# Attention kernel: the inverse softmax sums reach the head's partitions through a row in DRAM

## The chip, the cores and the metric

One core of one Trainium2 chip runs the whole program. The metric is device time in microseconds (us) of one launch, the median of three runs. The engines are named as in the profile: PE is TensorE, PEld its weight loads, DVE VectorE, ACT ScalarE, POOL GpSimd, SP SyncE, and SPq and POOLq are the issues of transfers from SP's and POOL's queues.

## The reference

Two layers, of which the first is "forgetting attention" and the second a gated recurrence. Only the attention is touched by the change. Cut to what matters, for 16 heads of width 64 over 2048 positions:

```python
s = einsum("bhqd,bhkd->bhqk", q, k) + cum[:, :, q0:q1, None] - cum[:, :, None, :q1]
p = softmax(where(causal, s, -inf), axis=-1)
o = einsum("bhqk,bhkd->bhqd", p, v[:, :, :q1])
return einsum("bse,ed->bsd", o * silu(gate), w_out)
```

Each query's softmax needs the sum of its exponentials. The kernel weighs the values with the exponentials themselves and multiplies by the inverse sum afterwards, together with the gate.

## The kernel before

The program is a row of stages: `project` (queries, keys, values, gate), `attend`, `merge`, `project`, `recur`. The change lies in `attend`, which takes about a third of the time.

`attend` works through 16 heads, two to a `pair`. A head has 16 blocks of 128 queries, one to a step, and two blocks make a group: 8 groups to a head, 128 in all. Block i meets only the keys up to its own (causal), so the steps of a head grow from one chunk of scores to four. All engines run over the same steps with fixed lags. For step s, PE computes the scores of block s (`score`), transposes the exponentials of block s - 3 (`turn`) and, in two halves over steps 2g + 5 and 2g + 6, multiplies the values with group g (`weigh`). DVE takes the scores out of PSUM and subtracts the high parts from the transposed blocks (`take`, `low`). ACT makes the exponentials with their sums and the high parts (`exps`, `high`). Values are split in a high and a low part throughout; `ops` has the high products on partitions 0 to 63 and the low ones on 64 to 127.

The sums of a group stand in `den`, one per query, hence one per partition, for two blocks (128 x 2). The product in `ops` has the queries along its columns (64 x 256), so the inverse sums have to be laid out along the columns and repeated on 64 partitions. Before the change this goes as follows. DVE inverts at step 2g + 3 (`invert`, L834). PE, at the end of `weigh`, transposes each inverse column, repeated 128 times, into the second half of `ops` (L716, two to a group). ACT, at the end of step 2g + 7, copies three tiles out of `ops` (`move`): the high product to `att` (L780), the low one to `low_sum` (L781), the spread inverse to `scale` (L782). POOL then does five operations of 64 x 256 per group: it adds the products (L641), multiplies `scale` by the gate (L643), writes the product twice (`yh` at L649, `y` at L650) and subtracts (`yl` at L652). The last of them counts up `y_ready`.

The couplings around it matter. `att`, `low_sum` and `scale` have two buffers, so `move` of group n waits for POOL to have finished group n - 2. SP issues every load and store of the stage from one queue, in order. For each group g it issues the gate tile of group g + 2 (L597), waits for `y_ready` of group g and stores `yh` and `yl` (L608, L609); after the first group of each head it also issues the nine transfers that load the whole next head (L586, L587). So the next head's load starts when POOL has finished group 0 of a head, and the gate tile of group 3 is the next thing in SP's queue behind it. POOL issues no transfers in this stage; in the first `project` it issues sixteen (L229), each of 16 rows of 2 KB.

Of the kernel before, what the change touches and what calls it, by code (L numbers as in the profile page):

```python
# [19 lines left out]
P = 128  # L20
BANK = 512
ALU = mybir.AluOpType
ACT = mybir.ActivationFunctionType
F32 = mybir.dt.float32
# [5 lines left out]
HEAD_DIM = 64  # L30
# [24 lines left out]
def raw(ap):  # L55

    return ap.bitcast(F32)
# [388 lines left out]
def wait(engine, sem, value):  # L446

    if not isinstance(value, int) or value > 0:
        engine.wait_ge(sem, value)
# [7 lines left out]
def attend(nc, stage, qs, ks, vs, gs, cum, ys):  # L457
# [13 lines left out]
    GW = 2 * P  # L471
    STEPS = 2 * QT
    GROUPS = 2 * GT
    PAIRS = D // HEAD_DIM // 2
# [17 lines left out]
    with ExitStack() as ctx:  # L492
        a = Alloc(nc, ctx, stage)
# [4 lines left out]
        val = [a.sb(f"val{i}", [P, QT, P], F32R) for i in range(2)]  # L498
# [1 line left out]
        ph = [a.sb(f"ph{i}", [P, QT, GW], F32R) for i in range(2)]  # L500
        pl = [a.sb(f"pl{i}", [P, QT, GW], F32R) for i in range(2)]
        gate = a.sb("gate", [HEAD_DIM, 4, GW])
        low_sum = a.sb("low_sum", [HEAD_DIM, 2, GW])
        scale = a.sb("scale", [HEAD_DIM, 2, GW])
        att = a.sb("att", [HEAD_DIM, 2, GW])
        y = a.sb("y", [HEAD_DIM, GW])
        yh = a.sb("yh", [HEAD_DIM, 2, GW], F32R)
        yl = a.sb("yl", [HEAD_DIM, 2, GW], F32R)
        least = a.sb("least", [P, ROWS, PB])
        den = a.sb("den", [P, 2, 2])  # L510
        rden = a.sb("rden", [P, 2, 2])
        ident = a.sb("ident", [P, P])
        identb = a.sb("identb", [P, P], BF16)
        mask = a.sb("mask", [P, P], BF16)
        sps = [a.ps(f"sps{i}", [P, BANK]) for i in range(SB)]
        tps = [a.ps(f"tps{i}", [P, PB, P]) for i in range(TB)]
        ops = [a.ps(f"ops{i}", [P, 2, GW]) for i in range(2)]

        waited = a.sem("waited")
        const_ready = a.sem("const_ready")  # L520
# [12 lines left out]
        low_out = a.sem("low_out")  # L533
        weighed = a.sem("weighed")
        rden_ready = a.sem("rden_ready")
        spread = a.sem("spread")
        moved = a.sem("moved")
        summed = a.sem("summed")
        scaled = a.sem("scaled")
        gated = a.sem("gated")  # L540
        y_ready = a.sem("y_ready")
# [81 lines left out]
        @block.gpsimd  # L623
        def _(pool):
            for t in (ident, identb, mask):
                nc.gpsimd.memset(t[:, :], 0.0).then_inc(const_ready, 1)
            pool.wait_ge(const_ready, 3)
            for t in (ident, identb):
                nc.gpsimd.affine_select(out=t[:, :], in_=t[:, :], compare_op=ALU.not_equal, fill=1.0, base=0,
                                        pattern=[[-1, P]], channel_multiplier=1).then_inc(const_ready, 1)  # L630

            nc.gpsimd.affine_select(out=mask[:, :], in_=mask[:, :], compare_op=ALU.is_ge, fill=MASKED, base=0,
                                    pattern=[[-1, P]], channel_multiplier=1).then_inc(const_ready, 1)

            def pair(it):
                for g in range(GROUPS):
                    n = it * GROUPS + g
                    b = g % 2
                    wait(pool, gate_loaded[g % 4], 16 * (it * (GROUPS // 4) + g // 4 + 1))
                    wait(pool, moved, 3 * n + 3)  # L640
                    nc.gpsimd.tensor_tensor(att[:, b, :], att[:, b, :], low_sum[:, b, :], ALU.add)\  # L641
                        .then_inc(summed, 1)
                    nc.gpsimd.tensor_tensor(scale[:, b, :], scale[:, b, :], gate[:, g % 4, :], ALU.mult)\  # L643
                        .then_inc(scaled, 1)
                    wait(pool, y_stored[b], 32 * (it * (GROUPS // 2) + g // 2))
                    wait(pool, scaled, n + 1)
                    wait(pool, summed, n + 1)
                    wait(pool, y_ready, n)
                    nc.gpsimd.tensor_tensor(yh[:, b, :], att[:, b, :], scale[:, b, :], ALU.mult).then_inc(gated, 1)  # L649
                    nc.gpsimd.tensor_tensor(y[:, :], att[:, b, :], scale[:, b, :], ALU.mult).then_inc(gated, 1)  # L650
                    wait(pool, gated, 2 * n + 2)
                    nc.gpsimd.tensor_tensor(yl[:, b, :], y[:, :], raw(yh[:, b, :]), ALU.subtract).then_inc(y_ready, 1)  # L652

            pair(0)
            for it in range(1, PAIRS):
                pair(it)

        @block.tensor
        def _(pe):
# [35 lines left out]
            def weigh(it, g, lo, hi):  # L695

                hp, gh, b = g // GT, g % GT, g % 2
                KT = 2 * gh + 2
                if lo == 0:
                    if isinstance(it, int) and it == 0 and hp == 0:  # L700
                        if gh % 2 == 0:
                            pe.wait_ge(first_val[gh // 2], 16)
                    elif gh == 0:
                        wait(pe, val_loaded[hp], 16 * (it + hp))
                    wait(pe, low_out, it * CH + first[2 * g + 1] + n_chunks[2 * g + 1])
                    wait(pe, moved, 3 * (it * GROUPS + g - 1))
                for kt in range(lo, hi):
                    c0 = P if kt == KT - 1 else 0
                    for t in (ph, pl):
                        mm = nc.tensor.matmul(ops[b][:, 0, c0:GW], val[hp][:, kt, :], t[b][:, kt, c0:GW],  # L710
                                              start=(kt == 0 and t is ph), stop=(kt == KT - 1 and t is pl))
                if hi == KT:
                    mm.then_inc(weighed, 1)
                    wait(pe, rden_ready, it * GROUPS + g + 1)
                    for e in range(2):
                        mm = nc.tensor.transpose(ops[b][:, 1, e * P:(e + 1) * P],  # L716
                                                 rden[:, b, e:e + 1].to_broadcast([P, P]), ident[:, :])
                    mm.then_inc(spread, 1)

            def step(it, s, begun):  # L720

# [33 lines left out]
        @block.scalar  # L755
        def _(act):
            def exps(it, s):

                i, g = s % QT, s // 2
                w = (i + 1) * P  # L760
                wait(act, scores_out, it * CH + first[s] + n_chunks[s])
                wait(act, rden_ready, it * GROUPS + g - 1)
                nc.scalar.activation(probs[s % ROWS][:, 0:w], probs[s % ROWS][:, 0:w], ACT.Exp,  # L763
                                     bias=least[:, s % ROWS, n_chunks[s] - 1:n_chunks[s]], scale=-1.0,
                                     accum_out=den[:, g % 2, s % 2:s % 2 + 1]).then_inc(probs_ready, 1)

            def high(it, s, j):
                i, g = s % QT, s // 2
                if j == 0:
                    wait(act, weighed, it * GROUPS + g - 1)  # L770
                c, n = first[s] + j, width(s, j) // P
                wait(act, turned, it * CH + c + 1)
                nc.scalar.activation(ph[g % 2][:, j * PB:j * PB + n, i % 2 * P:(i % 2 + 1) * P],  # L773
                                     tps[c % TB][:, 0:n, :], ACT.Copy).then_inc(high_out, 1)

            def move(it, g):
                b = g % 2
                wait(act, spread, it * GROUPS + g + 1)
                wait(act, y_ready, it * GROUPS + g - 1)
                nc.scalar.activation(att[:, b, :], ops[b][0:HEAD_DIM, 0, :], ACT.Copy).then_inc(moved, 1)  # L780
                nc.scalar.activation(low_sum[:, b, :], ops[b][HEAD_DIM:P, 0, :], ACT.Copy).then_inc(moved, 1)  # L781
                nc.scalar.activation(scale[:, b, :], ops[b][0:HEAD_DIM, 1, :], ACT.Copy).then_inc(moved, 1)  # L782

            def step(it, s, begun):

                def at(d, run):
                    n = s - d
                    if n >= 0 and n < STEPS:
                        run(it, n)
                    elif n < 0 and begun:  # L790
                        run(it - 1, n + STEPS)
                at(TURN_LAG, lambda t, n: [high(t, n, j) for j in range(n_chunks[n])])
                at(1, exps)
                if (s - TURN_LAG) % 2 == 0:
                    at(TURN_LAG + 3, lambda t, n: move(t, n // 2))

            for s in range(STEPS):
                step(0, s, False)
            for it in range(1, PAIRS):
                for s in range(STEPS):  # L800
                    step(it, s, True)
            for s in range(STEPS, STEPS + 3 + TURN_LAG):
                step(PAIRS - 1, s, False)

        @block.vector
        def _(dve):
# [23 lines left out]

            def invert(it, g):
                wait(dve, probs_ready, it * STEPS + 2 * g + 2)
                wait(dve, spread, it * GROUPS + g - 1)
                nc.vector.reciprocal(rden[:, g % 2, :], den[:, g % 2, :]).then_inc(rden_ready, 1)  # L834

            def step(it, s, begun):
                def at(d, run):
# [756 lines left out]
```

## Time and profile before

| | |
|---|---|
| median of 3 runs | 2558.09 us (2556.62 to 2558.27) |
| the profiled execution, its own time | 2556.05 us |
| its span, first to last instruction | 2553.9 us |
| attention, roughly | 770 to 1632 us of the span |
| PE busy in the whole span | 2409.2 us (94%) |
| POOL busy in the whole span | 622.7 us (24%) |
| one head, steady | 52.9 us, 15 times |

Busy shares are averages over stages. In a timeline each row is one instruction or a run of equal ones: its start, its duration, the engine, line and operation, and in brackets how long the engine sat idle before it and what ended that. PE's instructions overlap, so their pace is read from start to start and not from their durations.

### The profile page before, as it was taken

The page shows a single profiled execution, that of the slowest core. Times are in us where ns is not written, and L with a number is a line of the kernel's source. Part 1 is how long each engine was busy: PE and PEld are TensorE (multiplying, and loading weights), DVE is VectorE, ACT ScalarE, POOL GpSimd, SP SyncE. Part 2 cuts the span into 40 slices and gives each one's busy share as a digit, 9 for nine tenths or more (in the row PEclk, how much of TensorE's full clock was granted, in tenths as well). Part 3 has the DMA queues.
Part 4 walks back from the last instruction along what each step waited for, and adds up shares of the span by engine and source line. Part 5 has one row for each costly group of instructions (what it writes and reads, how often), then busy time and mean ns, then how long its engine had stood idle before and what let it go on. Part 6 is the DMA issues. An engine that isn't in the chain of part 4 may idle for free. (4 is left out here: it accounts for less than half of the span.)

```text
span 2553.9 us, 37956 instructions
## 1 busy us (share of the span) xinstructions
PE 2409.2 (94%) x13921; PEld 2081.5 (82%) x13921; DVE 1352.8 (53%) x2844; ACT 1150.0 (45%) x2132; POOL 622.7 (24%) x739
## 2 busy tenths in 40 slices
PE   8999999999989999999999999699699999992997
PEld 7888889998868888888888888587488888872886
DVE  4232121211017888888888888453336656575443
ACT  2131111111117888888888888400035556565100
POOL 0010000000003554555545555244300000000254
PEclk9999999999998999999999999899899999996999
DMA  6434443332116455444554444455344444444653
GB/s 209 122 91 124 124 124 113 119 108 91 66 61 136 98 122 131 104 98 98 128 128 102 97 99 96 147 203 194 124 153 122 142 144 132 139 125 139 236 193 132
DMA packets 219999, 326.62 MB, mean 128 GB/s; under 512 B 17052, under 2 KB 144092, under 8 KB 213996
## 3 DMA queue, kind: packets, MB, share of 16 engines
q1 hardware_dynamic: 219304, 323.68, 44.3%
q8 instruction: 111, 1.82, 0.3%
q0 software_dynamic: 512, 0.53, 0.1%
q14 instruction: 72, 0.59, 0.1%
HBM read 197.79 MB, written 126.35 MB: 127 GB/s over the span
## 5 line engine op out<-in xcount | busy, mean ns | idle before, releaser
L828 DVE TENSOR_TENSOR at_pl<-at_tps,at_ph 128x512 fp32r<-128x512 f32 (+3 forms) x640 | 370.7, 604 | 30.1 <-ACT at_ph L773 30.1
L773 ACT ACTIVATE at_ph<-at_tps 128x512 fp32r<-128x512 f32 (+3 forms) x640 | 311.5, 527 | 114.5 <-PE at_tps L692 107.4
L323 ACT ACTIVATE pa_stg<-pa_ps 128x512 fp32r<-128x512 f32 (+1 forms) x128 | 76.5, 598 | 634.9 <-PE pa_ps L250 634.9
L692 PE MATMUL at_tps<-at_ident,at_probs 128*128 128x128 f32 x2176 | 338.3, 274 | 0.2 <-DVE at_pl L828 0.2
L710 PE MATMUL at_ops<-at_ph,at_val 128*128 128x256 f32 (+1 forms) x1152 | 325.5, 305 | 2.1 <-DVE at_pl L828 0.5
L763 ACT ACTIVATE at_probs<-at_probs,at_least 128x128 f32<-128x128 f32 (+15 forms) x256 | 307.2, 1200 | 9.1 <-DVE at_probs L819 9.0
L250 PE MATMUL pa_ps<-pa_xh,pa_wh 128*128 128x512 f32 x768 | 299.8, 390 | 3.8 <-DVE pa_wl L376 3.8
L250 PE MATMUL pa_ps<-pa_xh,pa_wl 128*128 128x512 f32 x768 | 298.9, 389 | 0.0
L250 PE MATMUL pa_ps<-pa_xl,pa_wh 128*128 128x512 f32 x768 | 298.8, 389 | 0.0
L710 PE MATMUL at_ops<-at_pl,at_val 128*128 128x256 f32 (+1 forms) x1152 | 295.0, 281 | 0.0
L677 PE MATMUL at_sps<-at_k,at_q 128*128 128x512 f32 (+3 forms) x640 | 272.9, 426 | 19.9 <-DMA at_k<-forget_sums 15.8
L692 PEld LDWEIGHTS at_tps<-at_ident,at_probs 128*128 128x128 f32 x2176 | 256.6, 141 | 22.2 <-DVE at_pl L828 4.1
L819 DVE TENSOR_SCALAR_CACHE_REDUCE at_probs<-at_sps,at_least 128x512 f32<-128x512 f32 (+3 forms) x384 | 248.1, 646 | 16.4
L678 PE MATMUL at_sps<-at_k,at_q 68*128 68x512 f32 (+3 forms) x640 | 233.9, 369 | 0.0
L710 PEld LDWEIGHTS at_ops<-at_ph,at_val 128*128 128x128 f32 x1152 | 221.1, 192 | 12.8 <-DVE at_pl L828 4.4
L710 PEld LDWEIGHTS at_ops<-at_pl,at_val 128*128 128x128 f32 x1152 | 220.1, 191 | 8.3
L1301 PE MATMUL rep_ps<-rep_xh,rep_wh 128*128 128x512 f32 x512 | 201.4, 393 | 3.8 <-DVE rep_wl L1440 3.8
L1301 PE MATMUL rep_ps<-rep_xh,rep_wl 128*128 128x512 f32 x512 | 200.1, 391 | 0.0
L1301 PE MATMUL rep_ps<-rep_xl,rep_wh 128*128 128x512 f32 x512 | 200.0, 391 | 0.0
L959 PE MATMUL rem_ps<-rem_wh,rem_yin 128*128 128x512 f32 x512 | 160.6, 394 | 39.1 <-DMA rem_yin<-y_gated 39.1
L819 DVE TENSOR_SCALAR_CACHE_REDUCE at_probs<-at_sps 128x512 f32<-128x512 f32 (+3 forms) x256 | 162.0, 633 | 64.4 <-PE at_sps L678 60.8
L641 POOL TENSOR_TENSOR at_att<-at_att,at_low_sum 64x256 f32<-64x256 f32 x128 | 93.3, 729 | 385.7 <-ACT at_scale L782 221.7
(172 smaller groups left out, 4645.4 us busy)
## 6 DMA issues: line engine op xcount, KB each, us to landing
at_q<-q_halves SPq DMA_DIRECT2D x45, 512.0 KB
at_k<-k_halves SPq DMA_DIRECT2D x45, 512.0 KB
q_halves<-pa_stg SPq DMA_DIRECT2D x32, 512.0 KB, 3.8
k_halves<-pa_stg SPq DMA_DIRECT2D x32, 512.0 KB, 3.7
v_halves<-pa_stg SPq DMA_DIRECT2D x32, 512.0 KB, 2.8
y_gated<-rep_work SPq DMA_DIRECT2D x32, 512.0 KB, 2.9
at_val<-v_halves SPq DMA_DIRECT2D x15, 1024.0 KB, 17.4
pa_wst<-in_attn_w_in SPq DMA_DIRECT2D x14, 1024.0 KB, 7.2
```

Source lines behind the costliest of these rows:

```text
L250: mm = nc.tensor.matmul(out, lhs[p](c), rhs[q](c), start=(c == 0 and k == 0), stop=(c == KC - 1 and k == 2))
L641: nc.gpsimd.tensor_tensor(att[:, b, :], att[:, b, :], low_sum[:, b, :], ALU.add)\
L677: nc.tensor.matmul(out, q1[hp][:, i * P:(i + 1) * P], k1[hp][:, keys], start=True, stop=False)
L678: mm = nc.tensor.matmul(out, q2[hp][0:K, i * P:(i + 1) * P], k2[hp][0:K, keys], start=False, stop=not last)
L692: mm = nc.tensor.transpose(tps[c % TB][:, k, :], probs[s % ROWS][:, t0:t0 + P], ident[:, :])
L710: mm = nc.tensor.matmul(ops[b][:, 0, c0:GW], val[hp][:, kt, :], t[b][:, kt, c0:GW], start=(kt == 0 and t is ph), stop=(kt == KT - 1 and t ...
L763: nc.scalar.activation(probs[s % ROWS][:, 0:w], probs[s % ROWS][:, 0:w], ACT.Exp, bias=least[:, s % ROWS, n_chunks[s] - 1:n_chunks[s]], sc ...
L773: nc.scalar.activation(ph[g % 2][:, j * PB:j * PB + n, i % 2 * P:(i % 2 + 1) * P], tps[c % TB][:, 0:n, :], ACT.Copy).then_inc(high_out, 1)
L819: nc.vector.tensor_scalar(probs[s % ROWS][:, j * BANK:j * BANK + w], sps[c % SB][:, 0:w], 1.0, least[:, s % ROWS, j - 1:j] if j else None, ...
L828: nc.vector.tensor_tensor(pl[g % 2][at], tps[c % TB][:, 0:n, :], raw(ph[g % 2][at]), ALU.subtract)\
L959: mm = nc.tensor.matmul(psum[u][:, h, :], yin[n // 2 % 4][:, l, c, n % 2 * P:(n % 2 + 1) * P], w[:, c, h * BANK:(h + 1) * BANK], start=(c ...
L1301: mm = nc.tensor.matmul(psum[t % RING][:, :], wt[:, b, k, :], xt[:, k, at], start=(k == 0 and m == 0), stop=(k == KC - 1 and m == 2))
```

## The change

The transposes of the inverse sums on PE (L715 to L718) and the third copy on ACT (L782) go. In their place POOL issues two transfers per group: `store_rden` writes the inverse sums of a group (128 partitions x 2) to a row of 256 numbers in DRAM, and `spread_rden`, after the first has landed, reads that row onto 64 partitions of `scale`. POOL issues the store for group n + 1 at the head of its work on group n, and the spread for group n + 1 between its second and third operation on group n. PE no longer waits for `rden_ready`, and ACT's `move` waits for `weighed`. `att`, `low_sum`, `scale` and `rden` get four buffers, so that `move` of group n waits for group n - 4; `invert` waits until the store of group n - 4 has landed.

```diff
-        ops = [a.ps(f"ops{i}", [P, 2, GW]) for i in range(2)]
+        ops = [a.ps(f"ops{i}", [P, GW]) for i in range(2)]
+        row_scales = nc.dram_tensor("row_scales", (2, 2, P), F32, kind="Internal").ap()
...
+            def store_rden(n):
+                pool.wait_ge(rden_ready, n + 1)
+                pool.dma_start(row_scales[n % 2].rearrange("e p -> p e"), rden[:, n % 4, :], allow_slow_non_contiguous=True)\
+                    .then_inc(rden_stored[n % 2], 16)
+
+            def spread_rden(n):
+                pool.wait_ge(rden_stored[n % 2], 16 * (n // 2 + 1))
+                wait(pool, gated, 2 * n - 6)
+                pool.dma_start(scale[:, n % 4, :], row_scales[n % 2].rearrange("e p -> (e p)").partition_broadcast(HEAD_DIM))\
+                    .then_inc(rden_spread[n % 2], 16)
...
                 for g in range(GROUPS):
                     n = it * GROUPS + g
                     b = g % 2
+                    if n == 0:
+                        store_rden(0)
+                        spread_rden(0)
+                    if n + 1 < GROUPS * PAIRS:
+                        store_rden(n + 1)
                     wait(pool, gate_loaded[g % 4], 16 * (it * (GROUPS // 4) + g // 4 + 1))
-                    wait(pool, moved, 3 * n + 3)
+                    wait(pool, moved, 2 * n + 2)
+                    wait(pool, rden_spread[b], 16 * (n // 2 + 1))
...
+                    if n + 1 < GROUPS * PAIRS:
+                        spread_rden(n + 1)
...
                 if hi == KT:
                     mm.then_inc(weighed, 1)
-                    wait(pe, rden_ready, it * GROUPS + g + 1)
-                    for e in range(2):
-                        mm = nc.tensor.transpose(ops[b][:, 1, e * P:(e + 1) * P],
-                                                 rden[:, b, e:e + 1].to_broadcast([P, P]), ident[:, :])
-                    mm.then_inc(spread, 1)
...
-                wait(act, spread, it * GROUPS + g + 1)
-                wait(act, y_ready, it * GROUPS + g - 1)
+                wait(act, weighed, it * GROUPS + g + 1)
+                wait(act, y_ready, it * GROUPS + g - 3)
...
-                nc.scalar.activation(scale[:, b, :], ops[b][0:HEAD_DIM, 1, :], ACT.Copy).then_inc(moved, 1)
...
-                wait(dve, spread, it * GROUPS + g - 1)
-                nc.vector.reciprocal(rden[:, g % 2, :], den[:, g % 2, :]).then_inc(rden_ready, 1)
+                wait(dve, rden_stored[g % 2], 16 * ((it * GROUPS + g) // 2 - 1))
+                nc.vector.reciprocal(rden[:, g % 4, :], den[:, g % 2, :]).then_inc(rden_ready, 1)
```

## Rows read from the trace of the kernel before

**Rows 1.** The page: busy time by engine, then 40 slices of the span.

```profile
PE 2409.2 (94%) x13921; PEld 2081.5 (82%) x13921; DVE 1352.8 (53%) x2844; ACT 1150.0 (45%) x2132; POOL 622.7 (24%) x739
...
POOL 0010000000003554555545555244300000000254
PEclk9999999999998999999999999899899999996999
```

**Rows 2.** Busy time in stretches: 100 us of attention, then two parts of a head.

```profile
900.00:1000.00 100.00, 99.26 (x745) 89.13 (x743) 85.76 (x240) 86.11 (x182) 53.57 (x75) 1.00 0.48 109
...
841.00:865.00 24.00, 24.00 (x174) 21.63 (x173) 23.51 (x65) 20.70 (x40) 7.51 (x12) 1.00 0.93 199
865.00:894.00 29.00, 28.62 (x222) 25.61 (x221) 22.29 (x65) 25.04 (x59) 21.16 (x30) 1.00 0.15 38
```

**Rows 3.** Timeline of POOL over one head: start us, duration us.

```profile
840.43 0.73 POOL L652 TENSOR_TENSOR at_yl<-at_y,at_yh 64x256 fp32r<-64x256 f32 x1
...
864.83 0.73 POOL L641 TENSOR_TENSOR at_att<-at_att,at_low_sum 64x256 f32<-64x256 f32 x1 [10.86 <-DMA at_gate<-gate_path]
865.53 0.73 POOL L643 TENSOR_TENSOR at_scale<-at_scale,at_gate 64x256 f32<-64x256 f32 x1
867.89 0.73 POOL L652 TENSOR_TENSOR at_yl<-at_y,at_yh 64x256 fp32r<-64x256 f32 x1
868.59 0.73 POOL L641 TENSOR_TENSOR at_att<-at_att,at_low_sum 64x256 f32<-64x256 f32 x1
...
893.37 0.73 POOL L652 TENSOR_TENSOR at_yl<-at_y,at_yh 64x256 fp32r<-64x256 f32 x1
```

**Rows 4.** Timeline of SP's queue in the same head.

```profile
841.25 0.45 SPq L608 DMA_DIRECT2D y_halves<-at_yh  x1
...
845.57 0.60 SPq L586 DMA_DIRECT2D at_k<-k_halves  x1
...
846.87 0.25 SPq L586 DMA_DIRECT2D at_k<-forget_sums  x1
...
847.66 12.96 SPq L597 DMA_DIRECT2D at_gate<-gate_path  x1
```

**Rows 5.** Waits in the attention stage, 770 to 1640 us: total us, times, longest.

```profile
POOL at_att L641 <- ACT at_scale L782: 221.7, 97, 25.8
POOL at_att L641 <- DMA at_gate<-gate_path: 164.0, 15, 11.3
```

**Rows 6.** Timeline of PE at the end of a group.

```profile
1186.83 0.28 PE L710 MATMUL at_ops<-at_pl,at_val 128*128 128x128 f32 x1
1186.94 0.40 PE L716 MATMUL at_ops<-at_ident,at_rden 128*128 128x128 f32 x2
1187.18 0.60 PE L692 MATMUL at_tps<-at_ident,at_probs 128*128 128x128 f32 x4
```

**Rows 7.** Groups of instructions: count, busy us, mean ns, idle before.

```profile
L782 ACT ACTIVATE at_scale<-at_ops 64x256 f32<-64x256 f32 x128 | 48.4, 378 | 3.1
L834 DVE RECIPROCAL at_rden<-at_den 128x2 f32<-128x2 f32 x128 | 20.5, 160 | 9.9 <-ACT at_probs L763 9.9
```

**Rows 8.** The transfers that POOL issues at L229: durations ns min/median/max, then landing.

```profile
L229 POOL DMA_DIRECT2D forget_sums<-pa_fbuf x16: 484/487/672, 150.2 to 183.1; - x16
...
DMA to landing us min/median/max: 1.8/3.4/7.0
```

**Rows 9.** The page: DMA queues, packets, MB and share of 16 engines.

```profile
q1 hardware_dynamic: 219304, 323.68, 44.3%
...
q0 software_dynamic: 512, 0.53, 0.1%
```

**Rows 10.** Timeline of POOL, the last head's group 0 and the last group.

```profile
1581.85 0.73 POOL L652 TENSOR_TENSOR at_yl<-at_y,at_yh 64x256 fp32r<-64x256 f32 x1
...
1627.69 0.72 POOL L652 TENSOR_TENSOR at_yl<-at_y,at_yh 64x256 fp32r<-64x256 f32 x1
```

**Rows 11.** Timeline of PE: the first scores of the next head.

```profile
866.22 0.30 PE L677 MATMUL at_sps<-at_k,at_q 128*128 128x128 f32 x1
```

More of the change, by code:

```diff
@@ L502, in attend @@
         gate = a.sb("gate", [HEAD_DIM, 4, GW])
-        low_sum = a.sb("low_sum", [HEAD_DIM, 2, GW])
-        scale = a.sb("scale", [HEAD_DIM, 2, GW])
-        att = a.sb("att", [HEAD_DIM, 2, GW])
+        low_sum = a.sb("low_sum", [HEAD_DIM, 4, GW])
+        scale = a.sb("scale", [HEAD_DIM, 4, GW])
+        att = a.sb("att", [HEAD_DIM, 4, GW])
         y = a.sb("y", [HEAD_DIM, GW])
@@ L510, in attend @@
         den = a.sb("den", [P, 2, 2])
-        rden = a.sb("rden", [P, 2, 2])
+        rden = a.sb("rden", [P, 4, 2])
         ident = a.sb("ident", [P, P])
@@ L535, in attend @@
         rden_ready = a.sem("rden_ready")
-        spread = a.sem("spread")
+        rden_stored = [a.sem(f"rden_stored{i}") for i in range(2)]
+        rden_spread = [a.sem(f"rden_spread{i}") for i in range(2)]
         moved = a.sem("moved")
@@ L638, in pair @@
                     b = g % 2
+                    if n == 0:
[3 more added lines that the diff above has]
+                        store_rden(n + 1)
                     wait(pool, gate_loaded[g % 4], 16 * (it * (GROUPS // 4) + g // 4 + 1))
-                    wait(pool, moved, 3 * n + 3)
-                    nc.gpsimd.tensor_tensor(att[:, b, :], att[:, b, :], low_sum[:, b, :], ALU.add)\
+                    wait(pool, moved, 2 * n + 2)
+                    wait(pool, rden_spread[b], 16 * (n // 2 + 1))
+                    nc.gpsimd.tensor_tensor(att[:, g % 4, :], att[:, g % 4, :], low_sum[:, g % 4, :], ALU.add)\
                         .then_inc(summed, 1)
-                    nc.gpsimd.tensor_tensor(scale[:, b, :], scale[:, b, :], gate[:, g % 4, :], ALU.mult)\
+                    nc.gpsimd.tensor_tensor(scale[:, g % 4, :], scale[:, g % 4, :], gate[:, g % 4, :], ALU.mult)\
                         .then_inc(scaled, 1)
+                    if n + 1 < GROUPS * PAIRS:
+                        spread_rden(n + 1)
                     wait(pool, y_stored[b], 32 * (it * (GROUPS // 2) + g // 2))
@@ L648, in pair @@
                     wait(pool, y_ready, n)
-                    nc.gpsimd.tensor_tensor(yh[:, b, :], att[:, b, :], scale[:, b, :], ALU.mult).then_inc(gated, 1)
-                    nc.gpsimd.tensor_tensor(y[:, :], att[:, b, :], scale[:, b, :], ALU.mult).then_inc(gated, 1)
+                    nc.gpsimd.tensor_tensor(yh[:, b, :], att[:, g % 4, :], scale[:, g % 4, :], ALU.mult).then_inc(gated, 1)
+                    nc.gpsimd.tensor_tensor(y[:, :], att[:, g % 4, :], scale[:, g % 4, :], ALU.mult).then_inc(gated, 1)
                     wait(pool, gated, 2 * n + 2)
@@ L705, in weigh @@
                     wait(pe, low_out, it * CH + first[2 * g + 1] + n_chunks[2 * g + 1])
-                    wait(pe, moved, 3 * (it * GROUPS + g - 1))
+                    wait(pe, moved, 2 * (it * GROUPS + g - 1))
                 for kt in range(lo, hi):
@@ L709, in weigh @@
                     for t in (ph, pl):
-                        mm = nc.tensor.matmul(ops[b][:, 0, c0:GW], val[hp][:, kt, :], t[b][:, kt, c0:GW],
+                        mm = nc.tensor.matmul(ops[b][:, c0:GW], val[hp][:, kt, :], t[b][:, kt, c0:GW],
                                               start=(kt == 0 and t is ph), stop=(kt == KT - 1 and t is pl))
@@ L777, in move @@
                 b = g % 2
-                wait(act, spread, it * GROUPS + g + 1)
-                wait(act, y_ready, it * GROUPS + g - 1)
-                nc.scalar.activation(att[:, b, :], ops[b][0:HEAD_DIM, 0, :], ACT.Copy).then_inc(moved, 1)
-                nc.scalar.activation(low_sum[:, b, :], ops[b][HEAD_DIM:P, 0, :], ACT.Copy).then_inc(moved, 1)
-                nc.scalar.activation(scale[:, b, :], ops[b][0:HEAD_DIM, 1, :], ACT.Copy).then_inc(moved, 1)
+                wait(act, weighed, it * GROUPS + g + 1)
+                wait(act, y_ready, it * GROUPS + g - 3)
+                nc.scalar.activation(att[:, g % 4, :], ops[b][0:HEAD_DIM, :], ACT.Copy).then_inc(moved, 1)
+                nc.scalar.activation(low_sum[:, g % 4, :], ops[b][HEAD_DIM:P, :], ACT.Copy).then_inc(moved, 1)
             def step(it, s, begun):
```

## The prediction, as it was put on record before the change was run

> **What bounds the kernel now.** I read the page first. PE is busy in 94% of the span and POOL in 24% [rows 1], which makes PE look like the bound and POOL free. The share is an average, so I next cut the attention stage into stretches. Over 100 us of it PE is busy 99.26 us at full clock, DVE 85.76, ACT 86.11 and POOL 53.57 [rows 2]. PE sets the pace, and POOL is twice as full here as in the whole span. In the first 24 us of a head's cycle DVE reaches 23.51 us as well.
>
> Then I followed POOL through one head. Call "the ring" the way from one head's group 0 being finished on POOL to the next head's. It is finished at 841.16 (840.43 + 0.73) and at 894.10 (893.37 + 0.73): 52.94 us [rows 3]. The reader is to see two parts. In the first, up to 864.83, 23.67 us pass, and POOL does groups 1 and 2 and then sits 10.86 us until the gate tile of group 3 is there [rows 3]. The cause is SP's queue: 0.1 us after the group is finished SP starts to store it and then to issue the next head's load, and the gate tile behind it takes 12.96 us to issue [rows 4], while the DMA engines are busy 93% of the time [rows 2]. This happens 15 times, once for each head load [rows 5]. In the second part, from 864.83 to 894.10, 29.27 us, POOL does six groups (3 to 7 and the next head's 0). A group back to back takes 3.76 us (864.83 to 868.59) [rows 3], so six take 22.56 and 6.71 us are idle. That is all the slack POOL has, because the first part starts anew when group 0 is finished and its 23.67 us run from there. More buffers don't add to it: lag is carried over, since the next load starts as much later.
>
> **What is removed.** On PE, two transposes per group. Start to start they take 1187.18 - 1186.94 = 0.24 us, and matmuls stand on either side without a gap [rows 6]; 128 x 0.24 = 30.7 us, or 1.92 us per head, all on the path now as PE is full. DVE's 0.49 us of idle in the 24 us [rows 2] holds back a little of it, as three of the eight groups lie there; I take 1.7 to 1.9. On ACT a copy of 378 ns per group, 48.4 us in all [rows 7], off the path: ACT has 14% idle. It also brings `moved` 0.4 us earlier. Left alone, PE would make the ring about 51.1 us.
>
> **What is added: two issues on POOL per group.** No transfer of this shape is in the trace. The nearest is POOL's own at L229: 487 ns each for 16 rows [rows 8]. I take POOL to be unable to compute meanwhile, as it is an instruction in its order. The new store has 256 pieces of 4 bytes (neighbours in DRAM lie on different partitions), the spread 64 rows. The low bound is 0.49 us for each. The high bound goes by packets: L229's 16 transfers made 512 packets [rows 8, 9], 32 each with the ones that signal, so 15.2 ns a packet; 272 give 4.14 us and 80 give 1.22. Between them I go by how an issue grows on SP: 0.25 us for 2 rows, 0.60 for 64 [rows 4], 5.6 ns a row. From 0.487 that gives 0.487 + 240 x 0.0056 = 1.84 us for the store and 0.76 for the spread. It is another engine's slope, but the one measured slope there is, so I take it.
>
> **What is added: a wait for the store's landing.** The spread of group n + 1 waits on POOL for a store issued at the head of the same round, and the three operations that finish group n are queued behind it; for these wait SP's stores and, for group 0, the next head's load. While PE sets the pace this is hidden, for POOL waits for `moved` anyway. Once POOL is behind, only the store's own issue and two operations cover it (865.53 + 0.73 - 864.83 = 1.43 us) [rows 3]. Landing takes 1.8 us at least and 3.4 in the median [rows 8]. Least: 1.8 is under 0.49 + 1.43, no stall. Median: 3.4 - 1.92 = 1.48. Chosen: issue 1.84, the 1.31 between issue and landing of the quickest at L229, and 16 small packets on each DMA engine. A packet costs 0.443 x 16 x 2553.9 / 219304 = 82 ns [rows 9], so 1.3 us more: 4.45 us, less 1.84 + 1.43, a stall of 1.18. The spread's own landing is covered by the rest of the round (0.76 + 2.33 + 1.84 = 4.9 us).
>
> The Trainium skill (DMA: Bandwidth & Descriptors, Anatomy of one DMA, SWDGE path) gives a fixed cost of about 2.0 us for a small transfer issued from POOL; the trace has 1.8 to 3.4 [rows 8]. By 2.0 and the low issue the sum would be some 2540 us, as in the first rival below. The same page (Rules for kernel authors) says that a strided last dimension becomes one descriptor per element, which speaks against this store. By 256 descriptors the sum is the one below; with one for each of the 128 partitions a group would cost 6.2 us and the whole come to some 2645. No row here shows such a store.
>
> DVE's `invert` now waits for the store of group n - 4, which lies five rounds back on POOL: free until POOL lags by four groups, and then it waits together with `move`. The reciprocal is the same 160 ns [rows 7]. The new transfers carry 1 KB and 64 KB per group and are no load; I cost their bytes at nothing, and if they slowed the head load the 23.67 us would grow.
>
> **The sum.** Group 3 waits for its gate with the store of group 4 already issued, so it costs 3.76 + 0.76 = 4.52. The five others cost 3.76 + 1.84 + 0.76 + 1.18 = 7.54 each. The ring is 23.67 + 4.52 + 5 x 7.54 = 65.9 us against 52.94: 13.0 more, 15 times, 194 us. Groups 1 and 2 of a head fit into 23.67. In the last head seven groups follow with no load; they took 1628.41 - 1582.58 = 45.83 us [rows 10] and take 7 x 7.54 = 52.8, so 7 more. The profiled execution's 2556.05 us (2.0 under the median) becomes 2757; I say 2750. PE's 30 us vanish, because PE waits for POOL. A second ring gives no more: the load lands just before the gate tile, at about 23 us, and PE scores the new head at 866.22, 25.1 us in [rows 11], so a head load that starts late soon stalls PE too, but by less than POOL's own ring.
>
> **The rivals.**
> *POOL keeps up* (faster). At the lowest prices a group costs 3.76 + 0.98 = 4.74, group 3 4.25, and the ring is 23.67 + 4.25 + 23.7 = 51.6. That is 1.3 us less per head, 20 in all, with 1.7 in the last head: 2534 us. For it: the issues at L229 are short, and POOL waits 386 us in the stage [rows 5]. Against: it decides at 5.00 us per group ((52.94 - 27.92) / 5), which leaves 0.26 us for every stall and every piece beyond L229's.
> *Break-even.* Between 4.93 and 5.07 us a group the rings differ by under 0.35 us: 2551 to 2561.
> *Short issues, ordinary landing.* Issues 0.49, landing 3.4 us: a stall of 1.48 and 0.09 for the spread, 6.31 a group, ring 59.5: 98 us more, 2652.
> *Pieces cost by the packet.* 3.76 + 4.14 + 1.22 + 1.18 = 10.3 a group, ring 80.1: 407 us more and 26 in the last head, 2990.
>
> **How the numbers follow.** A measurement of this kernel tells about 0.2% (5 us) from no change. Chances: forecast, 2690 to 2860, 0.37; short issues with ordinary landing, 2590 to 2690, 0.20; by the packet, above 2860, 0.15; slower but under 2590, 0.05; break-even 0.05; POOL keeps up 0.18. Slower is then 0.77. The range goes from 2534, the best that the ring allows, to 2860: outside are the 0.15 above and about 0.03 below. The forecast's own range is 2690 to 2860.
>
> **What would show it.** Right: the heads' cycle is about 66 us, POOL's idle before L641 on `moved` is nearly gone after the gate tile of each head, the spread's issue waits about a microsecond for the landing of the store, and ACT waits at L780 for POOL's `yl`; PE's busy share in the stage falls to about 80%. Wrong: the store's issue is short or its landing is under 2.3 us; the gate tile comes much sooner than 23.67 us after group 0; POOL computes while a transfer is being issued; or the head's cycle is 51 us with PE still at 99%.

## The result, and the profile after

The changed kernel takes 3389.51 us in the median of four runs (3382.6 to 3390.47), the kernel before 2558.18 beside it: a ratio of 1.3245 (95% interval 1.3223 to 1.3268). It is 831 us slower. I had forecast slower with 0.77, but 2750 us, with a range up to 2860. Where a time below comes without a ratio, it is that of a single execution.

The page of the changed kernel, which answers to [rows 1] and [rows 9]:

```profile
span 3388.0 us, 37692 instructions
...
PE 2587.3 (76%) x13665; PEld 2217.0 (65%) x13665; DVE 1370.9 (40%) x2844; ACT 1135.8 (34%) x2004; POOL 783.7 (23%) x995
...
PE   9999999997575565655656656565379699999498
...
PEclk9999999998787776777777777686789899999799
...
q0 software_dynamic: 8704, 9.06, 1.7%
```

PE has fallen from 94% to 76% of a longer span, and the slices show where: the attention stage, in which PE had been full, now runs mostly at five to six tenths, and the granted clock in it falls to 0.6 to 0.8. Project, merge and the recurrence look as before. In the attention stage the waits, in total us, times and longest, say what PE and all others wait for:

```profile
POOL at_scale L647 <- DMA row_scales<-at_rden: 807.4, 117, 10.7
...
DVE at_rden L851 <- DMA row_scales<-at_rden: 417.0, 85, 10.3
...
PE at_sps L700 <- DMA at_k<-forget_sums: 261.1, 16, 20.0
POOL at_att L662 <- DMA at_scale<-row_scales: 137.9, 69, 7.9
...
POOL at_att L662 <- DMA at_gate<-gate_path: 76.3, 14, 9.2
...
POOL at_att L662 <- ACT at_att L798: 10.8, 4, 9.0
```

The first row is the answer. POOL waits 807 us, in 117 of 128 groups, for its own store of the inverse sums to land before it can issue the spread (L647). The wait for ACT's copies, 222 us in [rows 5], has shrunk to 11: POOL is always behind. DVE waits for the same stores at `invert` (417 us), and PE for head loads. ACT, which I had expected to wait at its first copy for POOL's `yl`, did so once, for 9.6 us: with four buffers the delay reaches DVE, ACT and PE through `invert`. One round of POOL, in the part of a head where only this pattern is left:

```profile
1267.56 0.76 POOL L640 DMA_DIRECT2D row_scales<-at_rden  x1
1268.85 0.72 POOL L662 TENSOR_TENSOR at_att<-at_att,at_low_sum 64x256 f32<-64x256 f32 x1 [0.53 <-ACT at_att L798]
1269.53 0.71 POOL L664 TENSOR_TENSOR at_scale<-at_scale,at_gate 64x256 f32<-64x256 f32 x1
1278.32 0.56 POOL L647 DMA_DIRECT2D at_scale<-row_scales  x1 [8.07 <-DMA row_scales<-at_rden]
...
1280.42 0.72 POOL L675 TENSOR_TENSOR at_yl<-at_y,at_yh 64x256 fp32r<-64x256 f32 x1
1281.08 0.76 POOL L640 DMA_DIRECT2D row_scales<-at_rden  x1
```

The store is issued at 1267.56 in 0.76 us. The two operations that can cover its landing are over at 1270.24. The spread is issued at 1278.32, 10.8 us after the store, and the next round begins at 1281.08: 13.5 us for a group that had cost 3.76 [rows 3]. In the median a round takes 12.6 us. Over the 117 groups that waited, the time from the store's issue to the spread's is 9.87 us in the median. I call this the landing from here on; it can be read in each run in the same way.

The other half of the ring got longer too. This is SP's queue behind a head load, to be held against the 12.96 us of [rows 4]:

```profile
1218.36 24.29 SPq L599 DMA_DIRECT2D at_gate<-gate_path  x1
```

From group 0 finished (1210.89 + 0.73 = 1211.62) to the start of group 3 (1246.80) it is now 35.2 us against 23.67. SP got past that issue at 1242.65. By itself this isn't the whole growth: POOL's own groups 1 and 2, each with its wait for a store, and the next store's issue lasted until 1242.95, 31.3 us, so 7.7 of the 11.5 us would have come with a gate tile in time, and POOL waited only 3.86 us more for it.

Why the gate tile is late shows in the traffic. First the changed kernel, in 4 us with a store out (issued at 1211.57, awaited until 1221.77) and the head load issued behind it, then in 4 us after it had landed and the next store had been issued, then in 4 us later on; below it the kernel before at the same place of a head. The columns are the stretch, PE, PEld, DVE, ACT and POOL busy, the clock, the DMA engines' busy share and GB/s:

```profile
1217.00:1221.00 4.00, 2.00 (x15) 1.71 (x14) 0.32 (x2) 2.85 (x6) 0.00 (x0) 1.00 0.83 35
1224.00:1228.00 4.00, 1.67 (x8) 1.27 (x7) 1.79 (x5) 0.60 (x1) 1.28 (x2) 0.50 1.06 244
...
1233.00:1237.00 4.00, 0.00 (x0) 0.00 (x0) 0.00 (x0) 0.00 (x0) 0.00 (x0) 0.50 0.90 102
```

```profile
847.00:851.00 4.00, 4.00 (x30) 3.50 (x29) 3.88 (x10) 3.73 (x10) 0.82 (x2) 1.00 1.05 225
```

35 GB/s against 244 and 225, at a busy share of 0.83: the engines are occupied and move little. The next store is issued at 1224.52, behind a full load. It is out in the second row too, and there the traffic holds; it dips some 9 us later (third row) before POOL sees that store land at 1239.45. So it isn't the mere presence of a store. That its pieces wait their turn behind the load and hold up the rest when it comes is my reading; no view shows single pieces. A head takes 104.6 us in the median of the 15, against 53.0.

### The profile page after: what moved, and what is told of

Its sections match the earlier page's. It is cut to its first block and busy times, and to the rows that moved or that the text cites. A ratio compares the mean times of both kernels' runs of the same rounds, so it can differ in the third digit from the quotient of the medians.

```text
span 3388.0 us, 37692 instructions
## 1 busy us (share of the span) xinstructions
PE 2587.3 (76%) x13665; PEld 2217.0 (65%) x13665; DVE 1370.9 (40%) x2844; ACT 1135.8 (34%) x2004; POOL 783.7 (23%) x995
## 3 DMA queue, kind: packets, MB, share of 16 engines
q1 hardware_dynamic: 219304, 323.68, 38.3%
q0 software_dynamic: 8704, 9.06, 1.7%
## 5 line engine op out<-in xcount | busy, mean ns | idle before, releaser
L700 PE MATMUL at_sps<-at_k,at_q 128*128 128x512 f32 (+3 forms) x640 | 329.5, 515 | 626.2 <-DVE at_probs L836 349.4
L700 PEld LDWEIGHTS at_sps<-at_k,at_q 128*128 128x128 f32 x640 | 151.0, 236 | 664.0 <-DVE at_probs L836 375.6
L715 PE MATMUL at_tps<-at_ident,at_probs 128*128 128x128 f32 x2176 | 407.2, 315 | 3.5 <-DVE at_pl L845 3.4
L733 PE MATMUL at_ops<-at_ph,at_val 128*128 128x256 f32 (+1 forms) x1152 | 363.5, 334 | 2.2 <-DVE at_pl L845 2.1
L733 PE MATMUL at_ops<-at_pl,at_val 128*128 128x256 f32 (+1 forms) x1152 | 327.1, 307 | 0.0
L715 PEld LDWEIGHTS at_tps<-at_ident,at_probs 128*128 128x128 f32 x2176 | 304.9, 164 | 32.4 <-issue 11.1
L701 PE MATMUL at_sps<-at_k,at_q 68*128 68x512 f32 (+3 forms) x640 | 276.3, 435 | 0.0
L733 PEld LDWEIGHTS at_ops<-at_ph,at_val 128*128 128x128 f32 x1152 | 255.5, 222 | 15.5 <-DVE at_pl L845 3.0
L647 POOL DMA_DIRECT2D at_scale<-row_scales x128 | 71.7, 560 | 823.0 <-DMA row_scales<-at_rden 807.4
L976 PE MATMUL ma_ps<-ma_wh,ma_yin 128*128 128x512 f32 x512 | 159.4, 392 | 67.3 <-DMA ma_yin<-y_halves 67.3
```

The source lines that it names most:

```text
L700: nc.tensor.matmul(out, q1[hp][:, i * P:(i + 1) * P], k1[hp][:, keys], start=True, stop=False)
L701: mm = nc.tensor.matmul(out, q2[hp][0:K, i * P:(i + 1) * P], k2[hp][0:K, keys], start=False, stop=not last)
L715: mm = nc.tensor.transpose(tps[c % TB][:, k, :], probs[s % ROWS][:, t0:t0 + P], ident[:, :])
L733: mm = nc.tensor.matmul(ops[b][:, c0:GW], val[hp][:, kt, :], t[b][:, kt, c0:GW], start=(kt == 0 and t is ph), stop=(kt == KT - 1 and t is pl))
L976: mm = nc.tensor.matmul(psum[u][:, h, :], yin[n // 2 % 4][:, l, c, n % 2 * P:(n % 2 + 1) * P], w[:, c, h * BANK:(h + 1) * BANK], start=(c ...
```

## The experiments

Four theories were to be told apart. A: the store's pieces are slow because they are many, small and side by side. B: any transfer issued from POOL lands late here. C: the transposes' removal did harm by itself. D: the ring through the head load and the gate tile, as I had predicted it, was the main limit. All edits are to the changed kernel unless it says otherwise.

**Without the transfers, and with the spread alone.** In the first, neither transfer is issued and `scale` comes from the gate tile alone; in the second the row is stored once.

```diff
-                    nc.gpsimd.tensor_tensor(scale[:, g % 4, :], scale[:, g % 4, :], gate[:, g % 4, :], ALU.mult)\
+                    nc.gpsimd.tensor_tensor(scale[:, g % 4, :], gate[:, g % 4, :], gate[:, g % 4, :], ALU.mult)\
...
-                    if n + 1 < GROUPS * PAIRS:
-                        store_rden(n + 1)
...
-                    if n + 1 < GROUPS * PAIRS:
-                        spread_rden(n + 1)
```

> The changed kernel without any of the 256 transfers: POOL squares the gate tile instead of multiplying it by the inverse sums, so the outputs are not normalised; POOL's five operations, ACT's two copies and PE's shorter groups stay. Both theories (slow store; slow transfers from POOL of any kind) expect PE to set the pace: a head's ring of about 51.1 us, 27 us less than before, 2527 to 2536 us by the profiled execution. If the removal of the transposes itself did harm, it would be at or above 2558.

Measured: 2543.76 us, ratio 0.9947 (0.9930 to 0.9963). C falls: the removal gives 13 us. It gives half of what I had forecast, and the time lies above the 2527 to 2536 that I had expected of this run. The heads take 52.0 us, 1.0 less, not 1.9. In the waits of the steady part (790 to 1580 us), the kernel before and then this run:

```profile
PEld at_sps L677 <- DVE at_probs L819: 11.8, 30, 0.5
```

```profile
PEld at_sps L692 <- DVE at_probs L828: 24.5, 77, 0.6
```

PE's weight loads now wait more than twice as often for DVE to take scores out of PSUM (77 times, not 30), 13 us more in all. DVE, at 23.51 of 24 us in the first part of a head [rows 2], is by this the next bound; no run made DVE's work lighter to show it.

> The row is stored once, for group 0, and every group spreads that same row (so all groups are scaled by group 0's sums): the spread's 128 issues and landings stay, the 127 other stores go. Theory A (the many small writes of the store are slow to be confirmed): a group costs POOL 3.76 + 0.56 = 4.3 us, its ring is 23.7 + 26 = 49.6 us, under PE's 51.1, so 2530 to 2545 us. Theory B (any transfer issued from POOL is slow to land here): the spread is late too, a group costs over 6 us and the time is over 2640 us.

Measured: 2553.94 us, ratio 0.9986 (0.9977 to 0.9996). B falls: 128 spreads of 64 KB issued from POOL leave the heads at 52.0 us. The 10 us over the first run, of which 9 are over the range I expected, lie outside the heads' cycle: the first group is finished 6.3 us later (its last operation starts at 793.84, not 787.59), since POOL first has to see a store land; the last one 3.6 us later; and PE's wait for the merge's first loads is 28.8 us and not 20.8.

**The stores without POOL's wait.** The spreads read another row, so POOL need not wait.

```diff
-                pool.wait_ge(rden_stored[n % 2], 16 * (n // 2 + 1))
...
-                pool.dma_start(scale[:, n % 4, :], row_scales[n % 2].rearrange("e p -> (e p)").partition_broadcast(HEAD_DIM))\
+                pool.dma_start(scale[:, n % 4, :], fixed_row.rearrange("e p -> (e p)").partition_broadcast(HEAD_DIM))\
```

> All stores and all spreads are issued, but the spreads read another row, stored once, and POOL doesn't wait for the stores (only DVE does, four groups later). If the store only takes long to be confirmed (pure latency), a group costs 3.76 + 0.76 + 0.56 = 5.1 us, the ring is 54 us, 2575 us. If the DMA engines also stand still while the small writes are out, eight stores of some 8 us and 21 us of head load no longer fit in 54 us: ring 85 to 105 us, 3050 to 3400 us.

Measured: 2980.67 us, a head 80.6 us in the median. POOL waits for no store here, yet 424 us are lost against the kernel before. That lies between my two expectations: more than latency alone, less than a full standstill. Where POOL and PE wait now:

```profile
POOL at_att L670 <- DMA at_scale<-fixed_row: 380.4, 66, 13.2
...
PE at_sps L708 <- DMA at_k<-forget_sums: 188.3, 15, 14.3
POOL at_att L670 <- DMA at_gate<-gate_path: 170.0, 13, 14.5
```

These are all other transfers that arrive late: the spread, which lands in time when it is alone, the head load and the gate tile. With POOL's wait for the store taken away, half of the loss stays, and it is what the stores do to everything else on the DMA engines. One wait for the stores is left, DVE's at `invert`; DVE sat idle there for 146 us in 44 groups, but POOL, whose rounds set the pace, waited only 46 us for ACT's copies, behind which DVE's work stands.

**The same pieces, farther apart.** The DRAM row gets a gap after each 4 bytes; POOL still waits for the store; the spread reads a row that was stored once. Only the step differs between the runs (512, 64, 32 and 8 bytes).

```diff
-        row_scales = nc.dram_tensor("row_scales", (2, 2, P), F32, kind="Internal").ap()
+        row_scales = nc.dram_tensor("row_scales", (2, 2, P, P), F32, kind="Internal").ap()
...
-                pool.dma_start(row_scales[n % 2].rearrange("e p -> p e"), rden[:, n % 4, :], allow_slow_non_contiguous=True)\
+                pool.dma_start(row_scales[n % 2, :, :, 0].rearrange("e p -> p e"), rden[:, n % 4, :], allow_slow_non_contiguous=True)\
```

> The store's 256 pieces of 4 bytes go to addresses 512 bytes apart, not side by side; POOL waits for the store as in the change, and the spread reads another row, stored once. If the writes are slow because they fall side by side in one 1 KB stretch and are done one after the other there, the store lands in 2.5 to 3.5 us, and the time is 2600 to 2680 us. If each small write is slow by itself on its DMA engine (16 in a row on each), the landing stays at 9 to 11 us and the time at 3300 to 3450 us.

> As the run with pieces 512 bytes apart, but 64 bytes apart. If the writes only hold each other up within 64 bytes, the time is that run's, 2600 to 2640 us, with the store landing in 2.7 us. If the stretch in which they meet is longer (256 or 512 bytes), the landing grows to 4 us and more and the time to over 2700 us.

Measured: 2615.07 us at 512 bytes and 2611.16 at 64, landing 2.67 us in both. Still 256 pieces of 4 bytes, still two issues and the wait on POOL, and 774 of the 831 us are gone. The traffic recovers too. These are, in the run at 512 bytes, SP's issue of the gate tile behind a head load (group 0 finished at 1134.55) and 4 us behind it with a store out (issued at 1139.91, awaited until 1149.09):

```profile
1140.88 13.15 SPq L601 DMA_DIRECT2D at_gate<-gate_path  x1
...
1141.00:1145.00 4.00, 4.00 (x30) 3.58 (x29) 3.88 (x10) 3.61 (x7) 0.77 (x2) 1.00 1.02 215
```

13.15 us and 215 GB/s, nearly as in the kernel before, where the changed kernel has 24.29 us and 35 GB/s. One round of POOL at 512 bytes, to be held against the one above:

```profile
1185.70 0.76 POOL L642 DMA_DIRECT2D row_scales<-at_rden  x1
...
1188.36 0.58 POOL L655 DMA_DIRECT2D at_scale<-fixed_row  x1 [0.43 <-DMA row_scales<-at_rden]
...
1191.17 0.76 POOL L642 DMA_DIRECT2D row_scales<-at_rden  x1
```

A round is 5.47 us. This run also tests the ring itself. In the median of its 15 heads the way to the gate tile takes 24.5 us, group 3 takes 4.2 and a later round 5.5, which makes 56.2; a head takes 56.5. The form of my sum was right and its price wrong.

> The store writes all 256 pieces of 4 bytes, one every 32 bytes, two to each 64 bytes; POOL waits for it, and the spread reads another row, stored once. If the delay grows with the number of pieces in 64 bytes, little is left of it: the store lands in 2.7 to 3.1 us, 2610 to 2660 us. If any two pieces in the same 64 bytes cost a fixed extra, it lands in 4 us or more, 2720 us and more.

> The store writes all 256 pieces of 4 bytes, one every 8 bytes, over 2 KB; POOL waits for it, and the spread reads another row, stored once. If small writes hold each other up within 64 bytes, there are 8 in each, as with the pieces of 8 bytes, and the landing comes down to 4 to 6.3 us: 2740 to 3050 us. If all 256 queue up behind each other, it stays at 9.9 us and 3300 to 3450 us.

Measured: 2628.74 us at 32 bytes, landing 2.84; 2823.63 at 8 bytes, landing 4.95. Two pieces in 64 bytes cost next to nothing, eight cost 2.3 us, sixteen 7.2. These four runs change a second thing, the row that the spread reads; the half row below shows that this isn't the cause, for there too the spread reads the other row, and the dense store still takes 8.28 us.

**Fewer pieces side by side.** First 128 pieces of 8 bytes in the same 1 KB (the row laid out query by query; POOL's product with the gate reads it in that order; nothing is left out). Then 128 pieces of 4 bytes, the first block's sums only, in 512 bytes, and the spread reads another row.

```diff
-                pool.dma_start(row_scales[n % 2].rearrange("e p -> p e"), rden[:, n % 4, :], allow_slow_non_contiguous=True)\
+                pool.dma_start(row_scales[n % 2], rden[:, n % 4, :])\
```

> The row in DRAM is laid out query by query, so the store has 128 pieces of 8 bytes instead of 256 of 4, side by side in the same 1 KB; POOL's product with the gate reads the spread row in that order. If each small write into the shared stretch costs its time after the other (some 8 us for 256, so 31 ns each), the store lands after about 6.3 us, a group costs POOL 9 us, and the time is 2900 to 3080 us. If it is a fixed penalty of the stretch, whatever the number, nothing changes: 3300 to 3450 us. If only pieces of under 8 bytes are slow, 2600 to 2680 us.

> The store writes only the first block's 128 sums (128 pieces of 4 bytes, side by side, over 512 bytes); POOL waits for it, and the spread reads another row, stored once. If small writes hold each other up within 64 bytes (16 pieces in each), the landing stays at 9.9 us and the time at 3300 to 3450 us. If all pieces of the row queue up behind each other, half of them take half: 6.3 us to land, 2900 to 3050 us.

Measured: 2748.89 us with 8 bytes, landing 4.14; 3210.88 with half a row, landing 8.28. None of my three expectations of the first holds (it lies between 2680 and 2900), and neither of the second. Half as many pieces, as dense as before, keep 5.6 of the 7.2 us over 2.67; half as dense, whether by size or by gaps, keep 1.5 and 2.3. Density decides most, and the number adds to it.

**The row in SBUF, and the head load in parts.** The row is a tile on one partition, again in pieces of 8 bytes, and nothing is left out; the second run also issues the next head's nine transfers in threes.

```diff
-        row_scales = nc.dram_tensor("row_scales", (2, 2, P), F32, kind="Internal").ap()
+        row_scales = a.sb("row_scales", [1, 2, GW])
...
-                    if g == 0:
-                        load_head(it, 1)
+                    if g < 3:
+                        load_head(it, 1, g)
```

> The row lies in SBUF, on one partition, and not in DRAM (128 pieces of 8 bytes, query by query); POOL's issues and waits stay. If slow confirmation belongs to DRAM, the store lands in some 2 us, a group costs 3.76 + 0.76 + 0.56 and up to 0.4 of stall, 5.1 to 5.5 us, a head's ring is 54 to 57 us, and the time 2560 to 2620 us: near the kernel before but not faster, since the ring of 5.0 us per group is exceeded. If small pieces are slow on any target, 2900 us and more.

> The same with the row in SBUF, and the next head's nine transfers are issued in three parts after groups 0, 1 and 2 of a head, not all after group 0, so that the gate tile and POOL's results don't stand behind all of them. If POOL's ring (the wait for the gate tile behind the head load) is what limited it, POOL needs 8 x 5.3 = 42 us of a head's 52 and PE and DVE set the pace again: 2540 to 2555 us, the gain of the run without transfers. If the ring is not the cause, it stays at the time of the run with the row in SBUF.

> The change as it is, with the next head's nine transfers issued in three parts after groups 0, 1 and 2. If POOL's wait for its own stores sets every group (8 groups of 12.3 to 13.5 us), the gate tile no longer matters and the time stays at 3300 to 3400 us. If the first part of the ring still counted as I had predicted, some 10 us per head go: 3200 to 3260 us.

Measured: 2600.79 us with the row in SBUF, ratio 1.0168 (1.0150 to 1.0185); 2553.5 with the load in parts as well, 0.9985 (0.9975 to 0.9994). So D is real once the store is fast: POOL's round is 5.5 us, above the 5.00 at which the ring decides, and taking the gate tile out of the queue is worth 47 us. In the change as it is, the same edit gives 3276.86 us, 113 less, between my expected 3200 to 3260 and 3300 to 3400. A head still takes 98.8 us. Its first part is 33.1 us in the median, against 35.9 in the changed kernel, since POOL's own groups 1 and 2 now fill it, and a round after group 3 takes 11.6 us against 12.4.

**The transposes put back.** The run without transfers, with PE's two transposes per group and their wait again, their result unused.

> The run without transfers (2543.8 us), with PE's two transposes per group put back and their result unused; ACT's third copy stays away, and the four buffers stay. If the 13.3 us that were gained come from the transposes, 2555 to 2559 us. If they come from ACT's copy or the deeper buffers, it stays at 2541 to 2547 us.

Measured: 2551.11 us, ratio 0.9982 (0.9972 to 0.9991). That lies between the two expectations. Of the 13.3 us, 7.4 are the transposes'. The other 5 or so (2 to 7 by the interval) come with what else differs from the kernel before, above all ACT's copy and the four buffers, which I had priced at nothing. A head takes 52.64 us here, 52.0 without the transposes, 52.96 before (of profiled executions; the one here was 3 us above its median).

**The transfers from SP's queue.** The row in SBUF and the load in parts, with store and spread moved from POOL's stream to SP's, the store two groups ahead.

```diff
+            def store_rden(n):
+                wait(sp, rden_spread[n % 2], 16 * (n // 2))
+                sp.wait_ge(rden_ready, n + 1)
+                sp.dma_start(row_scales[0:1, n % 2, :], rden[:, n % 4, :]).then_inc(rden_stored[n % 2], 16)
...
+                    if n + 1 < GROUPS * PAIRS:
+                        spread_rden(n + 1)
+                    if n + 2 < GROUPS * PAIRS:
+                        store_rden(n + 2)
                     wait(sp, y_ready, it * GROUPS + g + 1)
```

> The row in SBUF and the head load in three parts, as in the run at 2553.5 us, but store and spread are issued from SP's queue, the store two groups ahead, so that POOL is back at 3.76 us per group. If what kept that run 10 us above the run without transfers is POOL's time per group (5.4 us: two issues and the wait for the spread), this one comes to 2541 to 2548 us, faster than both kernels. If the transfers themselves or the split head load cost it, it stays at 2550 to 2556 us.

Measured: 2543.64 us, ratio 0.9950 (0.9936 to 0.9964). It leaves nothing out, beats both kernels, by 12 and 846 us, and equals the run that has no transfers at all. So what was left in the run at 2553.5 us was what store and spread cost on POOL, its two issues and its wait for the landing. 100 us of its attention, to be held against [rows 2]:

```profile
1100.00:1200.00 100.00, 98.83 (x729) 87.85 (x728) 87.97 (x245) 83.68 (x168) 54.24 (x76) 1.00 0.68 127
```

POOL's 54 us are those of the kernel before, and DVE has risen from 86 to 88.

## Why the prediction was wrong

**The bound before, and the ring.** Right in form. That POOL, idle for 76% of the span, would decide, and that it decides near 5 us per group, is borne out by the runs with a fast store: 5.4 to 5.5 us a round gives 56 to 57 us a head and 2600 to 2615 us in all, and cutting the ring gives it back. The rival that POOL keeps up failed for the reason given.

**What is removed.** The size was off: 1.7 to 1.9 us per head for the transposes, measured 0.64 (0.46 by the medians, 7.35 / 16). I had read PE's 99% as the whole bound and let DVE's 23.51 of 24 us hold back only a little; the waits of PE's weight loads for DVE doubled. That DVE is what holds it back is argued from these two numbers.

**Two issues on POOL.** 1.84 and 0.76 us taken, 0.76 and 0.56 measured. SP's slope per row does not carry over to POOL. This erred in the other direction, by 1.3 us a group.

**The store's landing.** This is the step that failed. I took 4.45 us from issue to landing, made of the issue, L229's least delay and 16 packets on each engine at the mean 82 ns. It was 9.87. The count was wrong: q0 has 8704 packets in the changed kernel and 4640 in the run with the spread alone, each with L229's 512, which gives 32 packets for a store and 32 for a spread, as for a transfer of 16 rows. That also takes the ground from the rival that priced 272 packets. And the mean was of the wrong kind: 323.68 MB in 219304 packets are 1.5 KB each, and they say nothing of 256 writes of 4 bytes into 1 KB. The runs with gaps show that neither the number nor the size of the pieces is slow in itself: at 64 bytes apart the same 256 land in 2.67 us, which is under what I had taken. The stall was 7.7 us a group (9.87 - 0.76 - 1.43), not 1.18.

**The bytes at nothing.** Also wrong, and I had named it as what would break the sum. The stores hold up the other traffic: the gate tile's issue went from 12.96 to 24.29 us, and the run in which POOL doesn't wait for them is still 424 us slower than before. With it fell the line that groups 1 and 2 of a head fit into 23.67 us: with their stores they took 31. With the measured terms the sum is 35.2 + 8.6 for group 3 (1246.80 to 1255.4) + 5 x (3.76 + 0.76 + 0.56 + 7.7 = 12.8) = 107.8 us a head, against 104.6 measured; 35.2 and 8.6 are of one head, and the medians of the 15 are 35.9, 6.6 and 12.4 a round.

The direction came out for the reason I gave, POOL's ring past its slack. But the 13.0 us a head that I had added were 51.6, so this is not a forecast that missed by a little.

The rule that I had cited from the Trainium skill (DMA: Bandwidth & Descriptors, Rules for kernel authors) warns of one descriptor per element; by the run with gaps those alone cost little here. The fixed 2.0 us that the Trainium skill gives (the same page, Anatomy of one DMA) fits the landing of 2.67 where the pieces don't meet, not the 9.87 where they do.

**Open.** Whether the writes wait in the memory or on their way to it isn't told by these traces: the density within some 64 bytes decides, and no run varied which DMA engine writes which piece. As gaps or size thin the pieces out, fewer partitions write into one stretch, and perhaps fewer engines; that this sharing, and not the count, is slow stays possible. No run issued the dense store to DRAM from SP's queue, so whether it would be as slow from there isn't known. Nor is it settled how the 5 us beside the transposes divide between ACT's copy and the four buffers.

## What to carry to other kernels

Price a small transfer by where its bytes land, not by their number: many 4-byte writes into the same few hundred bytes of DRAM took 10 us here and held up the other transfers, so put such a row in SBUF, or its pieces apart. An engine at a quarter of its time can still be the bound, if a ring of waits through it has a long stretch that it can't use; work out what each round may cost before adding to it. When the full engine gets lighter, look at the second fullest in each part of the cycle before counting the gain.

## What the hardware showed that I had not expected

Landing of 256 pieces of 4 bytes in DRAM, from issue to the waiting issue, median: 9.87 us side by side, 4.95 one every 8 bytes, 2.84 every 32, 2.67 every 64 and every 512. 128 pieces of 8 bytes side by side take 4.14, 128 of 4 bytes 8.28. With such a store issued just ahead of a head load, the core's DMA traffic fell to 35 GB/s, where the kernel before has 225 and the run with pieces 512 bytes apart 215. A store issued behind a head load lands late even with the pieces apart: 9.2 us (1139.91 to 1149.09 at 512 bytes).

A store of 256 scattered pieces occupies POOL for 0.76 us, one of 128 pieces for 0.60, a transfer of 16 rows for 0.49 [rows 8], one of 64 rows for 0.56: the issue grows little with the number of pieces.

PE's clock fell with its idle time. In 1224 to 1228 us of the changed kernel, where PE was busy 1.67 of 4 us, the granted clock was 0.50, the lower level of 1.2 GHz; from 1217 to 1221 it had still been 1.00, with PE busy 2 of 4 us (the rows of the traffic above). It isn't what sets the time here: POOL's rounds do, and POOL waited only 10.8 us for ACT's copies, behind which PE's work stands. From 900 to 1600 us the clock is 0.76 in the changed kernel and 0.97 in the run with pieces 512 bytes apart.
